# Weight sums of a Strassen-like up projection moved from the POOL engine into DRAM-to-DRAM accumulating transfers

## What is computed

```python
def conv_ffn(h, w_up, conv_w, conv_b, w_down, rows):
    bsz, length, _ = h.shape
    u = (h @ w_up).reshape(bsz, rows, length // rows, 2 * D_FF)
    up = jnp.pad(u, ((0, 0), (0, 0), (1, 1), (0, 0)))
    u = up[:, :, :-2] * conv_w[0] + up[:, :, 1:-1] * conv_w[1] + up[:, :, 2:] * conv_w[2] + conv_b
    a, b = jnp.split(u.reshape(bsz, length, 2 * D_FF), 2, axis=-1)
    return (jax.nn.silu(a) * b) @ w_down
```

## Time and profile before

| | us |
|---|---|
| three runs, median | 2885.37 |
| lowest, highest | 2881.08, 2885.82 |
| the profiled execution, its own time | 2889.67 |
| its span in the profile | 2887.9 |
| PE busy | 2715.0 (94%) |
| DVE busy | 1642.6 (57%) |
| ACT busy | 1177.1 (41%) |
| POOL busy | 455.2 (16%) |

### The profile page before, as it was taken

One profiled execution on the slowest core, in us unless ns is written; L12 is line 12 of the kernel. 1 busy time (PEld: TensorE's weight loads), 2 busy tenths in 40 slices (PEclk: granted clock), 3 DMA queues, 4 the chain that ended last, 5 costly groups with the idle time before them and its releaser, 6 DMA issues. The chain is left out here.

```text
span 2887.9 us, 42793 instructions
## 1 busy us (share of the span) xinstructions
PE 2715.0 (94%) x16764; PEld 2326.1 (81%) x16764; DVE 1642.6 (57%) x2842; ACT 1177.1 (41%) x2310; POOL 455.2 (16%) x546
## 2 busy tenths in 40 slices
PE   6999999999999999999999999999868888888999
PEld 6888888888998887877779888889756777776887
DVE  5766654445357666544464755543657777776334
ACT  5444443334245444433345612233544444444232
POOL 1221000000021210000020500000334333331000
PEclk9999999999999999999999999999889999999999
DMA  4112121111321122122132221123202222215131
GB/s 152 55 62 77 58 74 58 53 43 61 135 82 61 61 77 74 57 74 72 38 130 66 81 95 52 44 95 103 95 30 73 66 66 66 66 59 190 59 110 66
DMA packets 154375, 219.02 MB, mean 76 GB/s; under 512 B 9382, under 2 KB 117606, under 8 KB 154174
## 3 DMA queue, kind: packets, MB, share of 16 engines
q1 hardware_dynamic: 128064, 134.20, 14.8%
q0 software_dynamic: 26112, 82.08, 7.7%
HBM read 172.10 MB, written 42.02 MB: 74 GB/s over the span
## 5 line engine op out<-in xcount | busy, mean ns | idle before, releaser
L1036 PE MATMUL PS<-AH,WH 128*128 128x344 f32 (+2 forms) x2160 | 806.1, 373 | 43.0 <-DVE R L3087 18.8
L1036 PE MATMUL PS<-AL,WH 128*128 128x344 f32 (+2 forms) x2160 | 757.9, 351 | 0.0
L1036 PE MATMUL PS<-AH,WL 128*128 128x344 f32 (+2 forms) x2160 | 756.9, 350 | 0.0
L1036 PEld LDWEIGHTS PS<-AH,WH 128*128 128x128 f32 x2160 | 409.8, 190 | 102.4 <-issue 23.3
L1036 PEld LDWEIGHTS PS<-AH,WL 128*128 128x128 f32 x2160 | 409.0, 189 | 35.8
L1036 PEld LDWEIGHTS PS<-AL,WH 128*128 128x128 f32 x2160 | 410.6, 190 | 32.3 <-issue 1.0
L1036 PE MATMUL PS<-WH,AH 128*128 128x256 f32 (+1 forms) x1016 | 328.4, 323 | 12.2 <-issue 10.5
L1036 PE MATMUL PS<-WL,AH 128*128 128x256 f32 (+1 forms) x1016 | 327.4, 322 | 0.0
L1036 PE MATMUL PS<-WH,AL 128*128 128x256 f32 (+1 forms) x1016 | 327.1, 322 | 0.0
L2365 DVE TENSOR_TENSOR WL<-W,WH 128x1024 fp32r<-128x1024 f32 x140 | 172.3, 1234 | 185.7 <-ACT WH L1663 185.6
L2537 DVE TENSOR_REDUCE ST<-PS 128x1 f32<-128x784 f32 (+8 forms) x272 | 188.1, 733 | 142.6 <-PE PS L1036 142.2
(11 more groups left out here) (392 smaller groups left out, 4478.6 us busy)
## 6 DMA issues: line engine op xcount, KB each, us to landing
W<-in_k_w_in SPq DMA_DIRECT2D x66, 512.0 KB, 3.9
W<-in_w_ada SPq DMA_DIRECT2D x48, 512.0 KB, 4.9
W<-in_w_up SPq DMA_DIRECT2D x33, 512.0 KB, 4.3
W<-in_w_in SPq DMA_DIRECT2D x28, 512.0 KB, 3.8
W<-in_w_out SPq DMA_DIRECT2D x24, 512.0 KB, 3.5
W<-in_w_down SPq DMA_DIRECT2D x22, 512.0 KB, 3.8
s_gs<-R POOLq DMA_DIRECT2D x18, 512.0 KB, 3.5
R<-s_gs POOLq DMA_DIRECT2D x18, 512.0 KB, 8.2
```

The source lines that it names most:

```text
L1036: return e.matmul(out, lhsT, rhs, start=start, stop=stop, skip_group_check=True)
```

## The change

1. **Weight sums in DRAM.** A new DRAM scratch `wt` of four 512 x 2816 matrices holds the weights of products 5, 7, 6 and 4 (`WT_OF`). It is filled in 16 units of 128 rows by 704 columns. POOL issues for each unit four DRAM-to-DRAM copies and four accumulating DRAM-to-DRAM transfers, 352 KB each, spread over four steps. A step stands behind an `ada_out` that comes after a layer's last rotary multiplication: 14 steps in layer 0, 5 in layer 1, the last ones shorter.
2. **Loads.** SP loads each product's 256 KB block by itself, two for each slot, from `w_up` or `wt`; `combine_weights` is gone.
3. **ACT's and DVE's order in the up projection.** `snap` stands first in each step, ahead of the split and of what waits for DVE; `total` 11 stands ahead of `gate` on DVE; `taps` and `convolve` of (1,0) move a tile later.
4. **Activation sums.** s1, s2 and s4 have two buffers; pass 3 runs one step ahead. Products (1,1) and (1,2) now come before the transposes of pass 3 on PE (`if i == 3`), and splits 2 to 5 stand between the activation sums. Signs of some sums are turned, with the same number of operations.

```diff
+            def weight_sums(n):
+                w = A["w_up_2"][0]
+                if 1 <= n <= UNITS:
+                    e.wait_ge(*wt_copied.at(("wt", n - 1)))
+                if 2 <= n <= UNITS + 1:
+                    e.wait_ge(*wt_added.at(("wt", n - 2)))
+                if 3 <= n <= UNITS + 2:
+                    e.wait_ge(*wt_three.at(("wt", n - 3)))
+                if n < UNITS:
+                    top, low_, a, b = unit(n)
+                    e.dma_start(wt[0][top, a], w[top, a]).then_inc(*wt_copied.landed(("wt", n, 0)))
+                    e.dma_start(wt[1][top, a], w[top, b]).then_inc(*wt_copied.landed(("wt", n, 1)))
+                    e.dma_start(wt[2][top, a], w[low_, b]).then_inc(*wt_copied.landed(("wt", n, 2)))
+                    e.dma_start(wt[3][top, a], w[low_, a]).then_inc(*wt_copied.landed(("wt", n)))
+                if 1 <= n <= UNITS:
+                    top, low_, a, b = unit(n - 1)
+                    e.dma_start(wt[0][top, a], w[top, b], accum_op=ALU.add).then_inc(*wt_added.landed(("wt", n - 1, 0)))
+                    e.dma_start(wt[1][top, a], w[low_, b], accum_op=ALU.add).then_inc(*wt_added.landed(("wt", n - 1)))
+                if 2 <= n <= UNITS + 1:
+                    top, low_, a, b = unit(n - 2)
+                    e.dma_start(wt[2][top, a], wt[0][top, a], accum_op=ALU.add).then_inc(*wt_three.landed(("wt", n - 2)))
+                if 3 <= n <= UNITS + 2:
+                    top, low_, a, b = unit(n - 3)
+                    e.dma_start(wt[3][top, a], wt[2][top, a], accum_op=ALU.add).then_inc(*wt_four.landed(("wt", n - 3)))
...
                 turns = max(i for i, st in enumerate(STEPS[l]) if st[0] == "rope")
                 for at_, st in enumerate(STEPS[l]):
                     if st[0] == "ada_out":
...
+                        if at_ > turns:
+                            weight_sums(next(sums))
...
-            combine_weights(0, True)
-            combine_weights(0, False)
             for j in range(FT):
-                if j + 1 < FT:
-                    combine_weights(j + 1, True)
+                result(j)
                 if 1 <= j <= SPILL:
                     spill(j - 1)
-                result(j)
-                if j + 1 < FT:
-                    combine_weights(j + 1, False)
...
-                    for u, (j, ab) in enumerate(UP_LOADS):
+                    for u in range(UP_LOADS):
...
+                            e.wait_ge(*wt_four.at(("wt", UNITS - 1)))
                         else:
-                            jj, b = UP_LOADS[u - 4]
-                            e.wait_ge(*w_lo.at(("up", UP_AT[jj, 3 if b else 4])))
+                            e.wait_ge(*w_lo.at(("up", 2 * (u - 4) + 1)))
+                        for i in (2 * u, 2 * u + 1):
+                            e.dma_start(up_source(i).rearrange("p (a b) -> p a b", a=4), up_block(*UP_SEQ[i])).then_inc(
+                                *w_in[up_slot(u)].landed(("up", i)))
```

More of the change, by code:

```diff
@@ L1 @@
 from contextlib import ExitStack
+import itertools
 import numpy as np
@@ L2166, in combine_hi @@
                         e.wait_ge(*fill_tr.at(("ffn", 1, 7)))
[L2167 removed]
+                    e.activation(S_HI[name][:, k, c], CMB[name, k % 2], ACT.Copy).then_inc(*mix_hi.mark((name, p, k)))
             def up_split(i):
@@ L2175, in up_split @@
                     e.wait_ge(*gemm_mm.at(("up", i - 6)))
[L2176 to L2181, removed]
+                e.wait_ge(*w_in[up_slot(i // 2)].at(("up", i | 1)))
+                e.activation(up_half(i)[0], up_source(i), ACT.Copy).then_inc(*w_hi.mark(("up", i)))
             def mix_squares(q, p):
@@ L2242, in ffn @@
                 e.wait_ge(*cw_in.at(0))
-                up_split(2)
-                up_split(3)
-                for i, (j, p) in enumerate(UP_SEQ):
[L2246 to L2252, removed]
-                        snap(j, 1, C11)
[L2254 to L2266, removed]
+                e.wait_ge(*mix_dve.at((3, 3)))
+                snap(0, 1, C11)
+                snap(1, 1, C11)
+                combine_in(3, 0)
+                for k in range(4):
+                    if k < 3:
+                        combine_in(3, k + 1)
+                    combine_hi(3, k)
+                e.wait_ge(*mix_lo.at(("s4", 3, 3)))
+                for t in range(8):
+                    e.wait_ge(*stored("x1", t))
+                for i, (j, p) in enumerate(UP_SEQ):
+                    last = j - 1
+                    if p == 1 and j >= 2:
+                        if j == 2:
+                            convolve(1, 0, 0)
+                        e.wait_ge(*conv_v.at((j - 2, 0, 0)))
+                        snap(j, 1, C11)
                     elif p == 6:
@@ L2282, in ffn @@
                         snap(j, 7, C22)
+                    if 6 <= i + UP_AHEAD < len(UP_SEQ):
+                        up_split(i + UP_AHEAD)
+                    if p == 1 and j >= 3:
+                        convolve(last, 1, 0)
+                    elif p == 2 and j >= 3:
+                        gate(last)
+                    elif p == 2 and j == 1:
+                        convolve(0, 0, 0)
+                    elif p == 6:
+                        if j in (1, 2):
+                            convolve(last, 1, 0)
+                        if j >= 2:
+                            convolve(j, 0, 0)
+                    elif p == 5 and j in (1, 2):
+                        gate(last)
                     elif p == 3:
                         convolve(j, 1, 1)
-                        convolve(j, 1, 0)
                     elif p == 4:
@@ L3114, in ffn @@
                 e.wait_ge(*cw_in.at(0))
-                up_split_lo(2)
-                up_split_lo(3)
+                total(0, 11)
+                total(1, 11)
+                combine_sums(3, 0)
+                for k in range(4):
+                    if k < 3:
+                        combine_sums(3, k + 1)
+                    combine_rest(3, k)
                 for i, (j, p) in enumerate(UP_SEQ):
-                    if i + UP_AHEAD < len(UP_SEQ):
+                    last = j - 1
+                    if 6 <= i + UP_AHEAD < len(UP_SEQ):
@@ L3119, in ffn @@
                         up_split_lo(i + UP_AHEAD)
-                    if i == 0:
-                        for k in range(4):
-                            combine_sums(3, k)
-                            combine_rest(3, k)
-                    last = j - 1
                     if p == 1 and j >= 3:
                         taps(last, 0, 1)
+                    elif p == 1 and j == 2:
+                        taps(1, 0, 0)
                     elif p == 2:
+                        if j >= 2:
+                            total(j, 11)
+                        if j >= 3:
+                            taps(last, 1, 0)
+                        elif j == 1:
+                            taps(0, 0, 0)
+                    elif p == 6:
```

177 lines of the change are left out of this document (90 added, 87 removed).

## The result

The changed kernel took 2761.44 us (median of 4 runs, 2758.98 to 2766.63) against 2883.22 for the kernel before beside it (4 runs, 2880.48 to 2885.82): a ratio of 0.958, with a 95% interval of 0.9562 to 0.9598. That is 122 us less; 120 were forecast. The profiled execution took 2761.49 us with a span of 2759.7.

A forecast was written before the change was run, and what follows sets the result against it. It took PE to be bound in the up projection by ACT and DVE waiting for each other, slowed by POOL. Terms -99.5 - 23.6 + 3 = -120, from 2885.4 to 2765 us; range 2750 to 2813.

The forecast's parts named there:

- the stand ahead of product 7: Up projection: PE stands 3.06 us each tile because ACT and DVE wait for each other, slowed by POOL's additions.
- The tile: Up projection: seven products of 2.74 us without a PE stand, 19.2 us a tile in place of 23.92.
- From (0,5) to the down projection: Up projection from product (0,5) to the down projection's first matmul: 419.5 us in place of 519.0, 99.5 less.
- the tail: Between up and down projection: 9.5 us in place of 10.5, bounds 8 and 12.
- The activation sums: Pass 3: two buffers and one step ahead let (0,5) start 23.6 us earlier, bounds 17 to 26.
- The sums in DRAM: Attention: the 128 DRAM transfers cost 3 us in all, bounds 0 and 20.
- (d): Attention: a step's transfers take between 9.2 and 23 us; the middle, 13.8, was taken, so no wait.
- (a): Attention: POOL's issues take 0.54 us each, 4.3 us for eight, and cost nothing.
- (c): Attention: the store of `OTt`, which ACT awaits, queues behind up to eight DMAs: 0 to 10 us.
- Rival C: Attention: transfers over 22 us delay `ada_out`, then DVE and PE; T - 22 for each of 16 steps; chance 0.07.
- T: Attention: time a step's transfers take; above 22 us it costs, from 29.5 us the change is slower.
- Rival A: Up projection: a smaller wait replaces the removed one, 2.5 us a tile over 19 tiles, +48, 2813 us; chance 0.10.

The follow-up runs named there:

- order alone: Kernel before with only the new order of ACT, DVE and POOL in the up projection, from tile 3 on: 2791.98 us, ratio 0.968.
- twice the bytes: Kernel before with the 128 DRAM transfers issued but unused, each with twice the columns (704 KB): 2908.92 us, ratio 1.0095.
- one position: Kernel before with one ACT instruction, `convolve(j, 0, 0)`, moved behind the copy after product 6 from tile 3 on: 2838.61 us, ratio 0.9842.
- sums without the order: Changed kernel with the old order of ACT, DVE and POOL in the up projection restored from tile 3 on: 2786.39 us, ratio 0.9663 to the kernel before.

## Why the prediction was right, and where it was not

- **What bounds the kernel.** Right: the stand ahead of product 7 was a loop of two lists. The order alone removes it. The clause "slowed by POOL" was right too, and weightier than I thought, since taking the additions away shortens a tile by 3.8 us without the order. The prediction did not say that parts 1 and 3 mostly do the same work twice.
- **The tile.** 19.2 us forecast, 19.2 measured, 0.69 for a split but for one a tile. The layout of one tile holds: `gate` ends at 2300.90, 1.1 us before product 6 is complete and the copy after it starts; I had found 0.7.
- **From (0,5) to the down projection.** 419.5 forecast, 416.25 measured. The small waits in tiles 0 to 2, 2 us, did not appear; the tail was 7.9 and not 9.5 (my bound below was 8); the 0.7 between (0,6) and (0,7) and one slow start were there.
- **The activation sums.** 23.6 forecast, 16.4 measured. The direction was right and the size was off: the bounds 17 to 26 just miss it. The step that failed is "with two buffers and one step ahead the busiest engine sets it", with ACT as the busiest at 2.7 us. DVE is the one that sets it, with seven instructions, and I took its durations from the earlier trace rows, where POOL and DVE work in turn. Seven times 0.34 us would be 2.4; in the changed kernel two of the seven lasted about 0.94 us beside POOL's additions, DVE waited for POOL's copy of a22 besides (0.29 us, once 1.19), and the step was 3.5 to 3.8. The same row that I used against POOL's additions in the up projection, 1.78 in place of 0.69, speaks against this one.
- **The sums in DRAM.** 3 forecast, 0.6 measured (2.3 less to 3.5 more). (d) was a guess between 9.2 and 23 us, and it was luck that the 13.8 in the middle was close: the next step's wait would have ended after 13.2 to 15.5. (a) was right: the issues of a step start some 0.53 us apart, accumulating ones too (below), and no one waited for them. (c) named the path that costs once the bytes are doubled.
- **Rival C** was the right one to fear, but its path and its price were wrong. At T of 26 its formula gives 4 x 16 = 64 us, and 26 were measured; DVE never waited for a late `ada_out`, and PE stood for ACT's writes of `OTt` (22.7 us in the whole trace), where a store of `OTt` fell behind a step. The bytes of the change would have had to double to lose 26 us.
- **Rival A** did not come: nothing took the place of the removed wait.

The misses partly cancel: the sums gave 7 us less than forecast, the stretch behind them 3 more, and ahead of (0,1), where 3 us more were forecast, the profiled execution had 9 less. That the total came within 4 us of the forecast is in part luck.

## What to carry to other kernels

When PE stands for a PSUM copy, look at what stands ahead of the copy in its engine's list before looking at how much that engine has to do: in the kernel with the order alone DVE busy 88 of 100 us cost nothing, since every wait for it ended before the copy behind it was due. Double buffering between two engines that hold each other back brings less than the durations of their turn-taking promise; sum the busiest engine's list with the durations that it has when both run, and consider giving most of the work to the one, though here this brought only 1 us by the trace. At the border between two stages, look for the first operand of the next stage at the end of a long list of results that are needed later.

## What the runs showed of the hardware that I had not expected

The row of an accumulating DRAM-to-DRAM transfer is longer on POOL than that of a plain one, but it holds nothing back. One step of the changed kernel; L3253 is a plain copy, the four behind it accumulate:

```profile
404.30 0.52 POOL L3253 DMA_DIRECT2D s_wt<-in_w_up  x1
404.81 0.91 POOL L3256 DMA_DIRECT2D s_wt<-in_w_up  x1
405.36 1.22 POOL L3257 DMA_DIRECT2D s_wt<-in_w_up  x1
405.90 1.53 POOL L3260 DMA_DIRECT2D s_wt<-s_wt  x1
406.42 1.85 POOL L3263 DMA_DIRECT2D s_wt<-s_wt  x1
```

The duration grows with the place in the row, 0.91 to 1.85 us, yet the next issue starts 0.51 to 0.55 us later each time. With twice the bytes a plain `ada_out` that came right behind such a row at 523.36 us, 0.53 us after the last issue, was shown with 1.88 us as well. So the durations overlap and are not to be added up: the eight issues of this step, 402.65 us the first, take 5.6 us from the first start to the last end. Why they grow was not tried.

The lower clock did not follow every stand. With 2.9 us ahead of it product 7 lasted 4.6 us in the kernel before, part of it at 1.2 GHz; with 1.3 us (one position) and with 0.7 (sums without the order) it lasted 3.0, one matmul's start at most being late. In the stretches 2300 to 2400 us of both kernels the granted clock is 1.00. With the slow start counted, the stand cost 4.8 us a tile before and 1.6 with one position: cut to half, it cost a third.

Nine DVE instructions were faster than seven beside POOL's two additions, 12.7 us against 13.4 for pass 3, though POOL's copy of 0.40 us then took 4.2 twice.
